# Moving the activation operands of the matrix products by 32 or 96 bytes in SBUF

## The reference

```python
def _swiglu(h, w_gu, w_down):                  # D_MODEL 1024, D_FF 2816
    gate, up = jnp.split(h @ w_gu, 2, axis=-1)
    return (jax.nn.silu(gate) * up) @ w_down

def first_block(x, ...):
    for l in range(DEPTH):                     # DEPTH = 2
        x = x + 0.5 * _swiglu(_rms_norm(x, ffn1_norm[l]), ffn1_w_gu[l], ffn1_w_down[l])
        x = x + _hybrid_mixer(_rms_norm(x, mix_norm[l]), w_in[l], ..., w_pa[l], w_pb[l], w_out[l])
        x = x + 0.5 * _swiglu(_rms_norm(x, ffn2_norm[l]), ffn2_w_gu[l], ffn2_w_down[l])
    return _rms_norm(x, final_norm)

def second_block(x, ...):
    for l in range(DEPTH):
        h = _hybrid_mixer_2(_rmsnorm(x, pre_mix_norm[l]), ..., w_in[l], ..., w_out[l])
        x = x + _rmsnorm(h, post_mix_norm[l])
        h = _conv_glu_ffn(_rmsnorm(x, pre_ffn_norm[l]), ffn_up[l], ..., ffn_down[l])
        x = x + _rmsnorm(h, post_ffn_norm[l])
    return x
```

## Time and profile before

| | before |
|---|---|
| median of three runs | 2171.36 us |
| the profiled execution | 2171.4 us |
| its span, first to last instruction | 2169.4 us |
| mean granted TensorE clock over the span | 0.951 |
| busy: TensorE, weight loads, VectorE, ScalarE, GpSimd | 92%, 90%, 56%, 46%, 30% |
| matmuls | 15758 |
| HBM read | 311.71 MB, 144 GB/s over the span |

### The profile page before, as it was taken

One profiled execution on the slowest core, in us unless ns is written; L12 is line 12 of the kernel. 1 busy time (PEld: TensorE's weight loads), 2 busy tenths in 40 slices (PEclk: granted clock), 3 DMA queues, 4 the chain that ended last, 5 costly groups with the idle time before them and its releaser, 6 DMA issues.

```text
span 2169.4 us, 41175 instructions
## 1 busy us (share of the span) xinstructions
PE 1997.0 (92%) x15758; PEld 1947.2 (90%) x15758; DVE 1223.9 (56%) x1478; ACT 998.3 (46%) x1306; POOL 657.7 (30%) x595
## 2 busy tenths in 40 slices
PE   6999979999999999898999999978999889869997
PEld 6999979999999999898999988967999789769997
DVE  4545475665455554755654575526664564456665
ACT  5434444544344344454543464444544463445543
POOL 4651201246317610302365113313330006122320
PEclk9999889999999998999999989988999889989999
DMA  6545433455455444334454532203545322124544
GB/s 227 193 140 191 160 104 130 147 184 193 143 188 198 171 161 177 109 141 136 167 202 144 189 122 93 95 32 105 173 157 173 117 97 98 39 75 139 174 157 153
DMA packets 49213, 314.26 MB, mean 145 GB/s; under 512 B 5712, under 2 KB 6864, under 8 KB 19920
## 3 DMA queue, kind: packets, MB, share of 16 engines
q1 hardware_dynamic: 48960, 311.09, 41.8%
q10 hardware_dynamic: 144, 1.69, 0.2%
HBM read 311.71 MB, written 1.05 MB: 144 GB/s over the span
## 4 chain that ended last, share of the span: by engine, by line
PE 63%; issue 18%; DVE 8%; ACT 6%; POOL 4%; DMA 1%; ACTq 1%; DVEq 0%; SPq 0%; POOLq 0%
PE ps L542 17%; PE ps L544 17%; PE ps L543 17%; PE ps L857 3%; DVE conv L1875 2%; PE ps L547 2%; PE ps L548 2%; PE ps L549 2%; ACT conv L1160 2%; ACT w_hi L1109 2%; DVE w_lo L1567 1%; DMA raw<-in_in_dram 1%; POOL m L2197 1%; DVE v L2073 1%; POOL rope_tmp L2161 1%
## 5 line engine op out<-in xcount | busy, mean ns | idle before, releaser
L1567 DVE TENSOR_TENSOR w_lo<-raw,w_hi 128x2048 fp32r<-128x2048 f32 (+1 forms) x322 | 707.1, 2197 | 405.1 <-ACT w_hi L1109 403.6
L542 PE MATMUL ps<-xn,w_hi 128*128 128x256 f32 x2688 | 783.1, 291 | 44.1 <-DVE w_lo L1567 15.6
L543 PE MATMUL ps<-xn,w_hi 128*128 128x256 f32 x2688 | 772.0, 287 | 0.0
L544 PE MATMUL ps<-xn,w_lo 128*128 128x256 f32 x2688 | 771.3, 287 | 0.0
L1109 ACT ACTIVATE w_hi<-raw 128x2048 fp32r<-128x2048 f32 (+1 forms) x322 | 561.9, 1746 | 115.3 <-DMA raw<-in_down_dram 74.8
L542 PEld LDWEIGHTS ps<-xn,w_hi 128*128 128x128 f32 x2688 | 527.8, 196 | 56.8 <-issue 39.7
L543 PEld LDWEIGHTS ps<-xn,w_hi 128*128 128x128 f32 x2688 | 528.1, 196 | 0.6 <-issue 0.5
L544 PEld LDWEIGHTS ps<-xn,w_lo 128*128 128x128 f32 x2688 | 527.5, 196 | 0.0
L542 PE MATMUL ps<-h,w_hi 128*128 128x256 f32 x1056 | 297.2, 281 | 9.7 <-DVE conv L1875 5.1
L544 PE MATMUL ps<-h,w_lo 128*128 128x256 f32 x1056 | 295.4, 280 | 0.0
L543 PE MATMUL ps<-h,w_hi 128*128 128x256 f32 x1056 | 295.3, 280 | 0.0
(11 more groups left out here) (310 smaller groups left out, 2716.5 us busy)
## 6 DMA issues: line engine op xcount, KB each, us to landing
raw<-in_gu_dram SPq DMA_DIRECT2D x132, 1024.0 KB, 4.8
raw<-in_in_dram SPq DMA_DIRECT2D x70, 1024.0 KB, 4.9
raw<-in_down_dram SPq DMA_DIRECT2D x96, 704.0 KB, 4.0
raw<-in_out_dram SPq DMA_DIRECT2D x16, 1024.0 KB, 4.8
raw<-in_pb_dram SPq DMA_DIRECT2D x4, 1024.0 KB, 4.8
raw<-in_pa_dram SPq DMA_DIRECT2D x4, 1024.0 KB, 4.9
tables_all<-in_tables_dram ACTq DMA_DIRECT2D x1, 1648.0 KB, 7.0
rows<-in_rows_dram SPq DMA_DIRECT2D x2, 768.0 KB, 6.8
```

The lines of the kernel that those rows point to most:

```text
L542: pe.matmul(out, w, xh, start=first, stop=False)
L543: pe.matmul(out, w, xl, start=False, stop=False)
L544: return pe.matmul(out, wl, xh, start=False, stop=last)
L1567: dve.tensor_tensor(w_lo[:, r, 0:elems], raw[:, k % RAW_RING, 0:elems], w_hi[:, r, 0:elems], ALU.subtract).then_inc(lo.sem, 1)
```

## The change

The number, form and order of the instructions stay the same on every engine. What changes is where buffers lie.

- `xn` moves 32 bytes up, to 32 above a multiple of 128. The constants and small buffers behind it (from `tables_all` on) move with it.
- `area` is rounded up to a multiple of 128 rather than of 64. What lies at `area` itself and in its first 44 KB moves from remainder 64 to 0, and what lies behind that moves 128 bytes further, at remainder 0 too. The weights' rings and `x` do not move.
- Five moving operands get an offset of their own: `h`, `ya`, `yb` and `y2` lie 96 above a multiple of 128, `m` lies 32 above.

The core of the diff (the lines left out add the same `+ 128` to other buffers):

```diff
-XN_AT = X_AT + KC * T * 4
+XN_AT = X_AT + KC * T * 4 + 32
...
-    area = (cursor[0] + 63) // 64 * 64
-    h = at_byte("h", [FC, 2, T], area, F32R)
-    silu_gate = at_byte("silu_gate", [2, T], area + 44 * KB)
-    hv = at_byte("hv", [2, T], area + 46 * KB)
+    area = (cursor[0] + 127) // 128 * 128
+    h = at_byte("h", [FC, 2, T], area + 96, F32R)
+    silu_gate = at_byte("silu_gate", [2, T], area + 128 + 44 * KB)
+    hv = at_byte("hv", [2, T], area + 128 + 46 * KB)
...
-    ya = at_byte("ya", [WC, 2, T], area + 45 * KB, F32R)
+    ya = at_byte("ya", [WC, 2, T], area + 96 + 45 * KB, F32R)
...
-    yb = at_byte("yb", [WC, 2, T], area + 63 * KB, F32R)
+    yb = at_byte("yb", [WC, 2, T], area + 96 + 63 * KB, F32R)
...
-    m = at_byte("m", [KC, 2, T], area + 24 * KB, F32R)
+    m = at_byte("m", [KC, 2, T], area + 24 * KB + 32, F32R)
...
-    y2 = at_byte("y2", [KC, 2, T], area + 67 * KB, F32R)
+    y2 = at_byte("y2", [KC, 2, T], area + 128 + 67 * KB + 96, F32R)
```

More of the change, by code:

```diff
@@ L249, in program @@
     w_scale = fixed("w_scale", [DN_H])
-    area = (cursor[0] + 63) // 64 * 64
-    h = at_byte("h", [FC, 2, T], area, F32R)
-    silu_gate = at_byte("silu_gate", [2, T], area + 44 * KB)
-    hv = at_byte("hv", [2, T], area + 46 * KB)
-    v = at_byte("v", [KC, T], area + 53 * KB)
+    area = (cursor[0] + 127) // 128 * 128
+    h = at_byte("h", [FC, 2, T], area + 96, F32R)
+    silu_gate = at_byte("silu_gate", [2, T], area + 128 + 44 * KB)
+    hv = at_byte("hv", [2, T], area + 128 + 46 * KB)
+    v = at_byte("v", [KC, T], area + 128 + 53 * KB)
     tok = at_byte("tok", [6, NT, W], area)
@@ L262, in program @@
     u_t = at_byte("u_t", [WC, T], area + 40 * KB)
-    ki_t = at_byte("ki_t", [T], area + 44 * KB)
-    soft = at_byte("soft", [2, GROUP, T], area + 45 * KB)
+    ki_t = at_byte("ki_t", [T], area + 128 + 44 * KB)
+    soft = at_byte("soft", [2, GROUP, T], area + 128 + 45 * KB)
     p_t = at_byte("p_t", [2, GROUP, P], area + 24 * KB)
-    rope_tmp = at_byte("rope_tmp", [NT, W], area + 53 * KB)
-    mix_b = at_byte("mix_b", [NT, W], area + 53 * KB)
-    ya_v = at_byte("ya_v", [NT, W], area + 57 * KB)
+    rope_tmp = at_byte("rope_tmp", [NT, W], area + 128 + 53 * KB)
@@ L269, in program @@
+    mix_b = at_byte("mix_b", [NT, W], area + 128 + 53 * KB)
+    ya_v = at_byte("ya_v", [NT, W], area + 128 + 57 * KB)
     att = at_byte("att", [NT, W], area + 28 * KB)
-    work = at_byte("work", [NT, 2 * P], area + 61 * KB)
-    ya = at_byte("ya", [WC, 2, T], area + 45 * KB, F32R)
-    ws_raw = at_byte("ws_raw", [WC, P], area + 66 * KB)
-    yb = at_byte("yb", [WC, 2, T], area + 63 * KB, F32R)
-    ws_m = at_byte("ws_m", [WC, P], area + 71 * KB)
-    rows = at_byte("rows", [3, W], area + 73 * KB)
@@ L276, in program @@
-    ki_rope = at_byte("ki_rope", [NT, 2, HD], area + 79 * KB)
-    sm_raw = at_byte("sm_raw", [KC, HD + NH], area + 63 * KB)
+    work = at_byte("work", [NT, 2 * P], area + 128 + 61 * KB)
+    ya = at_byte("ya", [WC, 2, T], area + 96 + 45 * KB, F32R)
+    ws_raw = at_byte("ws_raw", [WC, P], area + 128 + 66 * KB)
+    yb = at_byte("yb", [WC, 2, T], area + 96 + 63 * KB, F32R)
+    ws_m = at_byte("ws_m", [WC, P], area + 128 + 71 * KB)
+    rows = at_byte("rows", [3, W], area + 128 + 73 * KB)
+    ki_rope = at_byte("ki_rope", [NT, 2, HD], area + 128 + 79 * KB)
@@ L278, in program @@
+    sm_raw = at_byte("sm_raw", [KC, HD + NH], area + 128 + 63 * KB)
     sm_hi = at_byte("sm_hi", [KC, HD + NH], area + 20 * KB, F32R)
     sm_lo = at_byte("sm_lo", [KC, HD + NH], area + 28 * KB, F32R)
-    m = at_byte("m", [KC, 2, T], area + 24 * KB, F32R)
[L283 to L286, removed]
-    y2 = at_byte("y2", [KC, 2, T], area + 67 * KB, F32R)
@@ L288, in program @@
-    dn_k = at_byte("dn_k", [DN_H, T], area + 67 * KB)
+    m = at_byte("m", [KC, 2, T], area + 24 * KB + 32, F32R)
+    conv = at_byte("conv", [2, 2, T], area + 128 + 48 * KB)
+    conv_in = at_byte("conv_in", [2, 2, T], area + 128 + 57 * KB)
+    sq8 = at_byte("sq8", [KC, T], area + 128 + 67 * KB)
+    hm = at_byte("hm", [KC, T], area + 128 + 44 * KB)
+    y2 = at_byte("y2", [KC, 2, T], area + 128 + 67 * KB + 96, F32R)
+    dn_k = at_byte("dn_k", [DN_H, T], area + 128 + 67 * KB)
     dn_q = at_byte("dn_q", [DN_H, T], area + 24 * KB)
@@ L291, in program @@
     z_t = at_byte("z_t", [DN_H, T], area)
-    dn_sq = at_byte("dn_sq", [DN_H, T], area + 61 * KB)
-    q_diag = at_byte("q_diag", [DN_H, T], area + 53 * KB)
-    gb = at_byte("gb", [2, DN_H, P], area + 53 * KB)
+    dn_sq = at_byte("dn_sq", [DN_H, T], area + 128 + 61 * KB)
+    q_diag = at_byte("q_diag", [DN_H, T], area + 128 + 53 * KB)
+    gb = at_byte("gb", [2, DN_H, P], area + 128 + 53 * KB)
     k_dec = at_byte("k_dec", [DN_H, P], area + 12 * KB)
@@ L297, in program @@
     rhs_v = at_byte("rhs_v", [NT, DN_H, P], area + 20 * KB)
-    a_t = at_byte("a_t", [NT, DN_H, P], area + 61 * KB)
+    a_t = at_byte("a_t", [NT, DN_H, P], area + 128 + 61 * KB)
     qk = at_byte("qk", [NT, DN_H, P], area + 40 * KB)
[L300 to L310, removed]
+    qg = at_byte("qg", [DN_H, P], area + 128 + 65 * KB)
+    gam = at_byte("gam", [NT, DN_H, P], area + 128 + 71 * KB)
+    beta_s = at_byte("beta_s", [NT, DN_H, P], area + 128 + 75 * KB)
+    u_inv = at_byte("u_inv", [NT, DN_H, P], area + 128 + 67 * KB)
+    t_inv = at_byte("t_inv", [NT, DN_H, P], area + 128 + 57 * KB)
+    lev_p = at_byte("lev_p", [NT, DN_H, P], area + 128 + 71 * KB)
+    lev_c = at_byte("lev_c", [NT, DN_H, P], area + 128 + 75 * KB)
+    w_neg = at_byte("w_neg", [DN_H, P], area + 128 + 75 * KB)
+    state = at_byte("state", [DN_H, P], area + 128 + 77 * KB)
+    v_new = at_byte("v_new", [NT, DN_H, P], area + 128 + 57 * KB)
+    o_t = at_byte("o_t", [DN_H, T], area + 128 + 61 * KB)
     o_sq = at_byte("o_sq", [DN_H, T], area + 20 * KB)
```

## The result

The changed kernel takes 2155.84 us (median of five runs, 2152.75 to 2159.71), the kernel before 2169.96 us in five runs. The ratio is 0.9936, 95% interval [0.9921, 0.9951]: faster, by 0.6%, and 55 us above the forecast of 2101. The profiled execution took 2159.71 us (before 2171.4).

What follows compares the result with a forecast made beforehand. The prediction took the matmul stream's pace on TensorE as the bound: 60.5 us from xn plus 17.5 from the others, 78.0, times 0.9 is 70, so 2171.4 - 70 = 2101 us; range 2073 to 2172.

Steps and rivals of the forecast that it cites:

- rival B: Wide matmuls: every offset but 0 is alike, so only xn gains, to 117.8 ns; 18 us saved, 2153 us; chance 0.22.
- What bounds the kernel: Whole kernel: TensorE's matmul stream, busy 92% of the span, is the bound; the change acts above all through its pace.
- step 3: Whole kernel: 90% of the 78.0 us saved on TensorE reaches the end, 70 us; mixer waits take some.
- The rule of two independent read ports: TensorE: weight loads take no SBUF read bandwidth from the running matmul, so placement would change the time by 0.
- How many steps: Wide matmuls at full clock that the new places affect: 9300 with xn and 4060 with the other operands.
- Step 1: Products with xn, moved from 0 to 32: step from 120.0 to 113.5 ns, 60.5 us of TensorE's time saved.
- The sign that the prediction had named for its failure: Products with xn: the forecast as a whole is wrong if their step stays at 117 ns or more.
- Step 2: Products with h, y, ya, yb (64 to 96) and m (64 to 32): from 117.8 to 113.5 ns, 17.5 us saved.
- Step 4: Down stage: weight slots keep up, 3.4 us per slot against 3.75 us of matmuls, 0.3 us to spare.
- Step 5: Engines writing the operands, and small matmuls: new places cost 0, within 4 us either way.
- Rival D: Wide matmuls: starts off a multiple of 64 add a fetch, slowing the kernel to 2200 or 2260 us; chance 0.19.
- A: The forecast case: both new offsets leave the slow patterns, step 113.5 ns, 2101 us, own range 2073 to 2120; chance 0.46.

Runs made afterwards that it cites:

- e2: The changed kernel with xn put back at distance 0 and the other operands left at their new places: 2170.34 us, ratio 1.0025 to the kernel before.
- e3: The kernel before with xn, h, m, y, ya and yb all placed 192 bytes (modulo 256) above the weight tiles: 2128.98 us, ratio 0.9826.
- f2: The kernel before with only raw, w_hi and w_lo moved 128 bytes down: 2134.37 us in one run, the kernel before beside it 2164.36.
- f1: xn, h, m, y, ya and yb used from 4 to 24 bytes into longer buffers, at distances off the 32-byte grid: 2166.47 us, a single time.

## Why the prediction was wrong

The range (2073 to 2172) held the time, and faster was right, but the forecast case was not the one that happened. The measured time lies at rival B's 2153, though not for B's reason.

- **What bounds the kernel, and that only the pace of the matmuls can move.** The second half held: the other engines' busy times did not change, the step's dependence on the place was there, and e2, e3 and f2 moved the time by it in both directions. The first half failed in one stage, see step 3.
- **The rule of two independent read ports in the Trainium skill** ("TensorE: Matmul & The Clock Gate", Part 2), by which nothing would change. The traces disagree: with only the weights moved, the step of `h` went from 117.8 to 113.3 ns and that of `xn` from 120.0 to 118.7 (f2).
- **How many steps.** 9300 and 4060 were forecast, 9107 and some 4000 were counted. Held.
- **Step 1, `xn` from 0 to 32 at 113.5 ns. This failed.** It measured 116.8, and 118.3 where weights move past `xn`: -26.3 us and not -60.5. The sign that the prediction had named for its failure, 117 ns or more, was missed by 0.3 ns.
- **Step 2, the others at 113.5 ns. This failed too, in sign.** 118.3 for `h`, `ya` and `yb`, 119.9 for `y`: +3.2 us and not -17.5. The bound of 120.0 had been kept on the losing side, and `y` nearly reached it. Both failed for one reason: "distance from the weights' remainder helps" was drawn from two points, 0 and 64, with a period of 128 assumed, so that 32 and 96 would be alike and `h` at 320 the same as 64. The sweep shows a period of 256, 113.3 as the usual step only at 192, and now and then at 64, and neither extends to the neighbours tried. The 113.5 of the earlier trace rows (113.3 in the trace's ns) belonged to 64 itself, the place that the change left.
- **Step 3, nine tenths reach the end. This failed.** 14.1 of 23.1 us did (61%), and 11.7 (51%) between the two profiled executions; in e3 it was 40 of 63.5 us (63%), the latter from the starts as above. About half of the 11.4 us lost between the profiled executions is the second block's gate and up stage: its 2000 steps of `xn` are 6 us shorter, the two stages together 0.4 us. The prediction took it for bound by TensorE because it read "97 of 100 us busy" in the earlier trace rows. The same row has the answer: 783 matmuls in 100 us are 7.8 per us, against 169 in 20 us in the first block's stage, which is 8.5 as the window counts them and 8.3 by the step of 120 ns. That VectorE had 69 of 100 us there did not show the bound either; it was a loop over ScalarE and VectorE, in which each waits for the other. A matmul of 283 ns covers a gap of 100 ns or more before the next one; the busy share hides it, the count does not. The rest of the loss lies mostly in the mixers, whose lengths went up by 4 us in one place and down by 5 in another between the two executions, and is not settled further.
- **Step 4, the slots keep up.** Held where it was asked, in the down stages: e3's went from 62.3 to 60.2 us, as 528 steps of 4.4 ns ask (2.3 us).
- **Step 5, the writers cost nothing.** Held.
- **Rival D**, slower because 32 and 96 cut a multiple of 64. Half right for the wrong operands: at 96 and 224 the step does rise, at 32 it falls. The cut alone does not decide: 160 cuts a multiple of 64 and stood at 117.3 or 118.7, 128 does not and stood at 118.6.
- **A sum that does not come out.** The prediction's own range for A ends at 2120 for a step of 116 ns. 9300 x 4.0 and 4060 x 1.8 ns are 44.5 us, x 0.9 = 40, so it should end at 2131. The outer range does not rest on it.

What stays open: why one distance has two paces. `ya` kept one pace through a layer and the other through the next, and in e3 `y` ran at 113.3 in one layer and at 117.8 in the other, so entry into a stage may choose; no run tested that. And why 192 is the low place: the runs show that it is, no run shows what in SBUF makes it so.

## What to carry to other kernels

Count matmuls per microsecond in a window before calling a stage bound by TensorE; a busy share of 97% hid slots that took 8% longer than their matmuls need (6.23 against 5.76 us). Where an effect of addresses is suspected, don't interpolate between two places: sweep them, one trace can hold six distances at once. And place the operand that moves by its distance to the weights, not by its own alignment.

## What the runs showed of the hardware

- With 256 moving columns and a 128-column weight load per matmul, both 4 bytes an element, at full clock, the step goes from 113.3 to 121.7 ns with the distance of the two operands in a partition, by what is left of it modulo 256. 192 is best (113.3 in most blocks of `xn` and `h` in e3 and of `h` in f2, else 117.8), then 32 (116.7 or 117.8). 64 reached 113.3 in part of the products of `ya` and `yb` and seldom elsewhere, and stood at 117.8 for nearly all of `xn`, `h`, `m` and `y`. 0 and 96 are worst on the 32-byte grid (120.0), 196 worst of all (up to 121.7).
- At half clock, and with 8 moving columns, nothing of this is seen (213.3 and 112 ns). In the changed kernel the product with 8 moving columns went on at half clock with 213.4 ns per step, so there the load alone takes as long as the wide product's step.
- No distance reached the weight load's own step of 111.7 ns.
- 4 bytes decide: `yb` had 113.3 at 192 (e3) and 120.0 or more at 196 (f1, one run).
